# Expert up biases from small loads of three rows, added by four products in four row groups

## The reference, cut to what matters

```python
hcat = xb @ w_up[e] + b_up[e]                  # 128 rows x 1024, w_up 1024 x 2048
y = clamped_swiglu(hcat) @ w_down[e] + b_down[e]   # w_down 1024 x 1024
def clamped_swiglu(hcat):
    gate, lin = hcat[:, :D_EXPERT], hcat[:, D_EXPERT:]
    gate = jnp.minimum(gate, 7.0); lin = jnp.clip(lin, -7.0, 7.0)
    return (lin + 1.0) * (gate * jax.nn.sigmoid(1.702 * gate))
```

## Time and profile before

| | |
|---|---|
| median of 3 runs | 1734.01 us (1733.99 to 1736.2) |
| profiled execution | 1735.64 us, its span 1733.5 us |
| TensorE, VectorE, ScalarE, GpSimd busy | 1637.6, 1478.0, 1103.7, 214.2 us |
| granted clock over the span | 0.975 |
| experts | from about 570 us to the end |

### The profile page before, as it was taken

One profiled execution on the slowest core, in us unless ns is written; L12 is line 12 of the kernel. 1 busy time (PEld: TensorE's weight loads), 2 busy tenths in 40 slices (PEclk: granted clock), 3 DMA queues, 4 the chain that ended last, 5 costly groups with the idle time before them and its releaser, 6 DMA issues.

```text
span 1733.5 us, 33793 instructions
## 1 busy us (share of the span) xinstructions
PE 1637.6 (94%) x12579; PEld 1331.7 (77%) x12580; DVE 1478.0 (85%) x1721; ACT 1103.7 (64%) x1078; POOL 214.2 (12%) x134
## 2 busy tenths in 40 slices
PE   7999899889896999999999999999999999999993
PEld 6778787778675778888888888888888888888882
DVE  5585677676586899999999999999999999999995
ACT  4533425333325777777777777777777777777772
POOL 0001111010103121111211111111211112111110
PEclk9999989999797999999999999999999999999997
DMA  6231101000338999999999999999999999999993
GB/s 200 73 101 55 30 15 30 9 21 15 104 133 279 373 386 365 383 380 378 373 359 385 375 383 372 372 376 375 380 361 376 377 377 375 361 378 377 380 368 111
DMA packets 207631, 473.33 MB, mean 273 GB/s; under 512 B 18701, under 2 KB 29403, under 8 KB 207355
## 3 DMA queue, kind: packets, MB, share of 16 engines
q1 hardware_dynamic: 197179, 442.74, 69.2%
q0 software_dynamic: 9792, 27.28, 7.1%
q10 hardware_dynamic: 576, 2.10, 0.3%
HBM read 454.35 MB, written 26.08 MB: 277 GB/s over the span
## 4 chain that ended last, share of the span: by engine, by line
PE 60%; DMA 4%; DVE 2%; issue 1%; ACT 1%; SPq 0%; DVEq 0%; POOLq 0%; ACTq 0%
PE bank L2183 19%; PE bank L2186 19%; PE bank L2184 18%; PE bank L2209 3%; DMA w_raw<-in_expert_w_up 2%; PE bank L2193 1%; DVE moe_w_lo L2169 1%; ACT moe_w_hi L2165 0%; DMA x<-sum_rows 0%; DMA moe_x_gathered<-hn_rows,moe_gather_rows 0%; DMA sum_rows<-moe_y,moe_scatter_rows 0%; DVE x L2663 0%; DVE moe_x_lo L2220 0%; PE bank L2201 0%; DVE moe_a_lo L2220 0%
## 5 line engine op out<-in xcount | busy, mean ns | idle before, releaser
L2169 DVE TENSOR_TENSOR moe_w_lo<-w_raw,moe_w_hi 128x2048 fp32r<-128x2048 f32 x384 | 867.9, 2287 | 46.7 <-ACT moe_w_hi L2165 45.2
L2165 ACT ACTIVATE moe_w_hi<-w_raw 128x2048 fp32r<-128x2048 f32 x384 | 735.9, 1917 | 124.7 <-PE bank L2186 109.2
L2183 PE MATMUL bank<-moe_w_hi,moe_x_hi 128*128 128x512 f32 x1024 | 406.0, 396 | 0.3 <-DVE moe_w_lo L2169 0.3
L2186 PE MATMUL bank<-moe_w_lo,moe_x_hi 128*128 128x512 f32 x1024 | 400.2, 391 | 0.0
L2184 PE MATMUL bank<-moe_w_hi,moe_x_lo 128*128 128x512 f32 x1024 | 399.6, 390 | 0.0
L2186 PEld LDWEIGHTS bank<-moe_w_lo,moe_x_hi 128*128 128x128 f32 x1024 | 192.6, 188 | 41.0
L2183 PEld LDWEIGHTS bank<-moe_w_hi,moe_x_hi 128*128 128x128 f32 x1024 | 192.7, 188 | 40.2 <-DVE moe_x_lo L2220 1.3
L2184 PEld LDWEIGHTS bank<-moe_w_hi,moe_x_lo 128*128 128x128 f32 x1024 | 192.9, 188 | 38.6
L2183 PE MATMUL bank<-moe_w_hi,moe_a_hi 128*128 128x512 f32 x512 | 208.2, 407 | 1.4 <-DVE moe_a_lo L2220 1.4
L2186 PE MATMUL bank<-moe_w_lo,moe_a_hi 128*128 128x512 f32 x512 | 201.0, 393 | 0.0
L2184 PE MATMUL bank<-moe_w_hi,moe_a_lo 128*128 128x512 f32 x512 | 200.3, 391 | 0.0
(11 more groups left out here) (343 smaller groups left out, 2078.8 us busy)
## 6 DMA issues: line engine op xcount, KB each, us to landing
w_raw<-in_expert_w_up SPq DMA_DIRECT2D x512, 512.0 KB, 8.1
w_raw<-in_expert_w_down SPq DMA_DIRECT2D x256, 512.0 KB, 9.4
proj_w_raw<-in_w_in SPq DMA_DIRECT2D x36, 384.0 KB, 3.3
mixer_bias_table<-in_att_bias SPq DMA_DIRECT2D x16, 256.0 KB, 2.7
x<-in_w_o SPq DMA_DIRECT2D x8, 512.0 KB, 6.6
sum_rows<-x SPq DMA_DIRECT2D x5, 512.0 KB, 4.0
x<-in_x ACTq DMA_DIRECT2D x4, 512.0 KB, 6.7
x<-in_x SPq DMA_DIRECT2D x4, 512.0 KB, 4.0
```

The costliest lines, as they stand in the source:

```text
L2165: act.activation(w_hi[:, j % RING, :], raw[:, j % RAW, :], ACT.Copy).then_inc(hi_w[j % RING], 1)
L2169: eng.tensor_tensor(w_lo[:, j % RING, :], raw[:, j % RAW, :], w_hi[:, j % RING, :].bitcast(F32), ALU.subtract)\
L2183: pe.matmul(out, s_hi[:, k, :], w_hi[:, j % RING, w], start=first, stop=False)
L2186: ins = pe.matmul(out, s_hi[:, k, :], w_lo[:, j % RING, w], start=False, stop=ends)
```

## The change

`biasb` and `selb` are gone. Four small DMAs per expert (`load_bias`, L2199) bring 3 rows of 512 bf16 numbers each to partitions 0, 32, 64 and 96 of a buffer `bias_rows`, of which there are two. One burst of four products (`add_biases`, L2209 of the changed kernel), each over 3 rows in its own group of 32 rows of TensorE, adds them: it closes the banks U00 and U01 of the expert, and opens the banks U10 and U11 of the same expert, whose products come afterwards. The last products of slot 7 close U10 and U11. SyncE waits in each expert n until `actd` is 2n, which is the second half of the activation of expert n - 1, then issues the four loads for expert n + 1, and then the weight loads of expert n.

```diff
@@ slot_matmuls: first product of a bank only where not begun @@
-                    first = k == 0
+                    first = k == 0 and not begun
@@
-        def add_bias(pe, e, B, key, col):
-            pe.matmul(B.tile(key)[:, :], selb[:, ds(e, 1), :].rearrange("p a s -> p (a s)"), biasb[:, col:col + 512],
-                      start=False, stop=True).then_inc(B.fill_sem(key), 1)
+        bias_view = bias_dram.rearrange("(a e) (g c) -> e g a c", a=3, g=4)
+
+        def load_bias(sp, e, buf):
+            for g in range(4):
+                sp.dma_start(brow[32 * g:32 * g + 3, buf, :], bias_view[ds(e, 1), g, :, :].rearrange("e a c -> (e a) c"))\
+                  .then_inc(bias_in[buf], 16)
+
+        def add_biases(pe, buf, loaded, B, it, first, B1, it1, second):
+            pe.wait_ge(bias_in[buf], 64 * loaded)
+            for key in second:
+                pe.wait_ge(B1.free_sem(key), B1.before(it1, key))
+            for Bk, key, g, ends in ((B, first[0], 0, True), (B, first[1], 2, True), (B1, second[0], 1, False),
+                                     (B1, second[1], 3, False)):
+                rows = slice(32 * g, 32 * g + 3)
+                ins = pe.matmul(Bk.tile(key)[:, :], ones[rows, :], brow[rows, buf, :], start=not ends, stop=ends)
+                if ends:
+                    ins.then_inc(Bk.fill_sem(key), 1)
@@ pe_block @@
-                slot_matmuls(pe, n, j, B, it, keys, x_hi, x_lo, 2 * (j - 4))
+                slot_matmuls(pe, n, j, B, it, keys, x_hi, x_lo, 2 * (j - 4), keys if j == 7 else (), True)
-            for i, key in enumerate(keys):
-                add_bias(pe, e, B, key, F * i + 512)
@@
-                for i, key in enumerate(first):
-                    add_bias(pe, e + 1, B, key, F * i)
+                add_biases(pe, 1 - par, it + par + 1, B, it, first, B, it + par, [(1 - par, "U10"), (1 - par, "U11")])
@@ act_block, ahead of the split of slot 11 @@
+            act.wait_ge(B.fill_sem((par, "U11")), B.count(it, (par, "U11")))
+            act.sem_inc(used[3], 1)
@@ SyncE, start of the experts @@
-            sp.dma_start(biasb[:, :], bias_dram).then_inc(bias_in, 16)
-            sp.dma_start(selb[:, :, :], ext["c_selb"].bitcast(BF16).rearrange("p (e s) -> p e s", e=E)).then_inc(bias_in, 16)
+            load_bias(sp, 0, 0)
+            load_bias(sp, 1, 1)
@@
-            with sp.Fori(1, E - 1) as n:
-                load_block(sp, n, n, True)
+            with sp.Fori(0, E // 2 - 1) as i:
+                for q in range(2):
+                    n = 2 * i + 1 + q
+                    sp.wait_ge(actd, 2 * n)
+                    load_bias(sp, n + 1, q)
+                    load_block(sp, n, n, True)
@@ GpSimd, start @@
+            pool.memset(ones[:, :], 1.0).then_inc(ones_set, 1)
```

More of the change, by code:

```diff
@@ L2069, in experts @@
         ident = keep["ident"]
-        posm, meta, over, biasb, selb, iota, lim = (keep[k] for k in ("posm", "meta", "over", "biasb", "selb", "iota", "lim"))
+        posm, meta, over, iota, lim = (keep[k] for k in ("posm", "meta", "over", "iota", "lim"))
         x, dense, counts, order, raw = (keep[k] for k in ("x", "dense", "counts", "order", "w_raw"))
@@ L2091, in experts @@
         fs = sb("final_sums", [P, NT + 1])
+        brow = sb("bias_rows", [P, 2, 512], BF16)
+        ones = sb("ones", [P, P], BF16)
         nov = sb("overflows", [P, E])
@@ L2118, in experts @@
         fw_in = sem("final_w_in")
-        bias_in = sem("bias_in")
+        bias_in = [sem(f"bias_rows_in{b}") for b in range(2)]
+        ones_set = sem("ones_set")
         bd_filled = sem("own_bias_filled")
@@ L2170, in split_lo, with slot_matmuls @@
                .then_inc(lo_w[j % RING], 1)
-        def slot_matmuls(pe, n, j, B, it, keys, s_hi, s_lo, k0, finish=()):
+        def slot_matmuls(pe, n, j, B, it, keys, s_hi, s_lo, k0, finish=(), begun=False):
             pe.wait_ge(lo_w[j % RING], nslot(n, j) + 3)
@@ L2418, in first_pe @@
                 slot_matmuls(pe, 0, j, pro, 0, keys, x_hi, x_lo, 2 * j)
-            pe.wait_ge(bias_in, 32)
-            for i, key in enumerate(keys):
-                add_bias(pe, 0, pro, key, F * i)
+            pe.wait_ge(ones_set, 1)
+            pe.wait_ge(bd_done, NT)
+            add_biases(pe, 0, 1, pro, 0, keys, main, 0, [(0, "U10"), (0, "U11")])
             pe.wait_ge(bd_done, NT)
@@ L2521, in lead_in @@
                     slot_matmuls(eng, n, j, B, it, keys, x_hi, x_lo, 2 * j)
-                for i, key in enumerate(keys):
-                    add_bias(eng, e, B, key, F * i)
+                add_biases(eng, 0, it + E // 2 + 1, B, it, keys, B, it, [(0, "U10"), (0, "U11")])
             if what == "act":
@@ L2599, in _ @@
                         e = sp.value_load(over[0:1, ds(k, 1)], min_val=0, max_val=E - 1)
+                        sp.wait_ge(actd, 2 * (E + k))
+                        load_bias(sp, e, 0)
                         load_lead_in(sp, E + k, e)
@@ L2723, in router_constants @@
     tri = np.concatenate([1.0 * (p[:, None] < p[None, :]), np.ones((P, P))], axis=1)
-    selb = np.zeros((3 * E, E, P))
-    for part in range(3):
-        selb[E * part + np.arange(E), np.arange(E), :] = 1.0
     b16 = lambda v: (v.astype(np.float32).view(np.uint32) >> 16).astype(np.uint16)
-    return {"c_router": rc, "c_lim": lim, "c_tri": b16(tri), "c_selb": b16(selb.reshape(3 * E, E * P)),
+    return {"c_router": rc, "c_lim": lim, "c_tri": b16(tri),
             "c_iota": np.arange(T + P, dtype=np.float32) + 1.0}
@@ L2764, in build @@
         mix_router(nc, psum, ext, keep, hn_dram, acc_dram)
-        for name, shape, dt in (("over", [P, 2 * NOV + 1], I32), ("biasb", [3 * E, 2 * F], BF16), ("selb", [3 * E, E, P], BF16),
-                                ("final_w", [P, D], F32)):
+        for name, shape, dt in (("over", [P, 2 * NOV + 1], I32), ("final_w", [P, D], F32)):
             keep[name] = sb(name, shape, dt)
```

## The result

The changed kernel takes 1862.63 us (median of 4 runs, 1857.56 to 1864.69), the kernel before, on the same chip, 1735.11 us (4 runs, 1733.99 to 1738.07). The ratio is 1.073, 95% interval 1.071 to 1.075. The sign of the forecast was right, its size was half of what came: 1798 was predicted, 64 us more, and it is 128 us more, outside the range.

The account below looks back on a forecast made before the run. Taken as bound by TensorE with the DMA right behind; a turn of 7.2 + 25.0 + 5.7 = 37.9 us, 30 times, against 1073.0 before adds 64 to 1734, giving 1798 us, range 1752 to 1832.

Parts of the forecast that it names:

- S: The DMA's service time per expert, taken as 35.6 us, just under TensorE's 35.72.
- The place of the loss: SyncE's wait before the next expert's first load leaves a DMA queue hole of 2.3 us in every expert.
- T: The moment the second half of an expert's activation ends, for which SyncE waits in the changed kernel.
- I take 5.2, bounds 4.9 and 6.7: Microseconds from issue to landing of the first pair of weight loads behind the wait, on idle DMA engines.
- Worse: Rival: TensorE's clock falls while idling, 1876 us, or the pair takes 6.7 us to land, 1843; chance 0.06.
- From slot 12 to T: From slot 12's landing over ScalarE's split, VectorE's split and the activation to T: 5.7 us a turn.
- TensorE is not in this loop: Claim that the turn from T to T bypasses TensorE, so its saved 0.6 us a turn buys nothing.
- The eight slots: Weight loads queued behind an expert's first load, up to slot 12: 25.0 us of each turn.
- Elsewhere even: Two 1.15 MB start loads gone, about 3 us, against eight small issues added, 2.7 us: even.
- The signs: Expected in the profile: ScalarE's splits wait 1 to 3 us an expert for DMA; SyncE's longest wait at L2199.
- The burst: TensorE's four bias products: 0.30 us replacing 0.90, a gain of 0.6 us an expert, 19 us were TensorE alone.
- Nothing moves: Rival: the queue's hole is just filled and the DMA's S caps the gain, 1731 to 1734 us; chance 0.05.

Follow-up runs that it names:

- e5: Kernel before with every w_down load cut to 768 of its 1024 columns, not computing the layer's result: 1731.46 us.
- e2: Changed kernel with SyncE waiting for the first half of the activation instead of the second, and the burst's products reordered: 1735.71 us.
- e4: Changed kernel with the loads of slots 4, 5 and 6 issued ahead of SyncE's wait and the four bias loads: 1737.86 us.
- e9: Changed kernel with the loads of two slots, 4 and 5, issued ahead of SyncE's wait and the bias loads: 1738.95 us.
- e6: e2 with every w_down load cut to 768 of its 1024 columns, not computing the layer's result: 1714.17 us.
- e1: Kernel before plus only SyncE's wait for the second activation half ahead of an expert's first weight load, biases as before: 1807.01 us.
- e12: e1 with slot 4 loaded alone, the loads of slot 5 and all behind held until slot 4 has landed: 1940.61 us.
- e7: e6 with all four products of the burst reading rows 0 to 2, so in one row group: 1737.05 us.
- e8: Changed kernel with the load of one slot, slot 4, issued ahead of SyncE's wait and the bias loads: 1789.32 us.
- e10: Kernel before plus SyncE's wait for the second activation half, placed behind the load of slot 4, biases as before: 1733.36 us.

## Why the prediction was right, and where it was wrong

**What bounds the kernel now: right.** TensorE with the DMA right behind. Less work for the DMA alone (e5) or for TensorE alone (e2, e4, e9) leaves the time within 0.4% of before; less for both lowers it (e6). S, taken as 35.6, is 35.8 to 35.9 in e2, e4 and e9.

**The place of the loss: right.** It is the loop through SyncE's wait. The wait alone makes 72 us (e1); three slots queued ahead of it take all but 3 us away (e4). The bias loads harm through their 1.8 us of SyncE's time behind the wait, not through the DMA (e2, e4). The Trainium skill (DMA: Bandwidth & Descriptors, "Rules for kernel authors") speaks against small transfers for their overhead on the DMA; e2 has all of them and takes no longer, and their packets take 0.04 us an expert, so here that price isn't on the path.

**Cost of a bias load's issue: right.** 0.45 was taken, 1.8 for four; from T to the weight issue it is 2.06 for 1.99.

**"I take 5.2, bounds 4.9 and 6.7": the step that failed.** The pair lands 7.0 us after its issue in the turn shown, 6.85 in the mean, beyond the upper bound. The value was put together from a lone load of 384 KB, 3.2 us, and bytes at the full rate. The row that was right stood beside it: the start at 544.1, 6.7 us, dismissed as the cold start of the weights, though each hole in the queue is such a start. In its place: 1.4 us until the first packet, two at 280 GB/s, and 0.6 for sharing with the loads behind (e12). It makes 1.6 of the 2.3 us by which a turn was too short, 30 × 1.6 = 48 us. The rival "Worse" had this price, 1843, and a chance of 0.06 together with the clock; it deserved far more.

**From slot 12 to T: 5.7 was too small, 6.4 measured,** 0.7 a turn, 21 us. Slot 12 lands at 1028.7, but ScalarE begins its split at 1029.41, behind X1, and X1 waits for TensorE, which waited for VectorE:

```profile
1027.49 0.68 DVE L2237 TENSOR_TENSOR moe_x_lo<-bank,moe_x_hi 128x512 fp32r<-128x512 f32 x1
```

```profile
1028.23 0.66 PE L2226 MATMUL bank<-ident,moe_x_gathered 128*128 128x128 f32 x4 [3.55 <-DVE moe_x_lo L2237]
```

```profile
1028.92 0.60 ACT L2231 ACTIVATE moe_x_hi<-bank 128x512 fp32r<-128x512 f32 x1 [0.99 <-PE bank L2226]
1029.41 1.90 ACT L2168 ACTIVATE moe_w_hi<-w_raw 128x2048 fp32r<-128x2048 f32 x1
```

The 5.7 is what the way takes when X1 is not late. So it is in 8 of the 30 turns (5.67 to 5.69); one is the turn whose slot 12 lands at 868.4 and whose T is 874.08:

```profile
867.53 0.58 ACT L2231 ACTIVATE moe_x_hi<-bank 128x512 fp32r<-128x512 f32 x1
868.50 1.91 ACT L2168 ACTIVATE moe_w_hi<-w_raw 128x2048 fp32r<-128x2048 f32 x1 [0.39 <-DMA w_raw<-in_expert_w_up]
```

In the other 22 turns X1 ends after slot 12 has landed, and the way takes 6.3 to 6.9. The forecast's "TensorE is not in this loop" was therefore not quite so: its transposition is, though not its products.

**The eight slots: right,** 24.9 for 25.0. **Elsewhere even: off by 5 us,** to the good: expert 0's T came 4.7 us earlier. Together 48 + 21 - 5 is 64, the whole miss. **The signs:** SyncE's longest wait and the hole behind T are where the forecast put them; but the splits wait for loads for (117.9 + 21.9) / 15 = 9.3 us an expert (1000 to 1600 us), where it said 1 to 3.

**The burst: right in kind, dearer than taken.** 0.30 was taken. Four products in four row groups take 0.33 us, and with the 0.09 ahead of them 0.42; so the gain is 0.90 - 0.42 = 0.48 an expert instead of 0.6, 15 us, and e6 against e5 gives 0.49 an expert, 17.3 us in all. That it needs distinct row groups is shown by e7. The Trainium skill (TensorEngine Tiling (Array Packing), "Key Properties") says that a change of the tiling mode drains the array; the rows agree, with 0.32 to the burst's start where 0.23 is usual, and with the same 0.32 in e7; that it is a drain they don't show.

**The clock.** The forecast said 1.00. After the 3.55 us without work TensorE ran at its lower level (1.2 GHz):

```profile
1026.00:1028.00 2.00, 0.00 (x0) 0.00 (x0) 2.00 (x2) 1.91 (x1) 0.00 (x0) 1.00 1.05 392
1028.00:1030.00 2.00, 1.77 (x8) 1.48 (x9) 2.00 (x3) 1.08 (x2) 0.00 (x0) 0.71 1.06 397
1030.00:1032.00 2.00, 2.00 (x6) 1.55 (x5) 2.00 (x3) 1.80 (x2) 0.00 (x0) 0.50 1.03 410
1032.00:1034.00 2.00, 2.00 (x10) 1.62 (x9) 2.00 (x2) 0.68 (x1) 0.00 (x0) 0.94 1.03 410
```

A mean of 0.71, 0.50 and 0.94 in three stretches of 2 us is 1.2, 2.0 and 0.2 us at 0.50, together 3.4. Behind it ScalarE waits 1.5 and 0.8 us for TensorE at slots 13 and 14, which are behind slot 12 and so outside the loop; how much of this is the clock and how much TensorE's late start isn't separated. To the way from slot 12 to T the clock adds next to nothing: in four turns it is 1.00 in the 20 us ahead of T (815.0 to 834.9, for one), and they take 6.4 to 6.6 us, like the others with a late X1.

**Rival "Nothing moves" is what the change does once the hole is covered:** e2, e4 and e9 stand at ratios of 1.0007, 1.0018 and 1.0034, none under 1. No version that computes the result is faster than the kernel before: e10's 1733.36 and e2's 1735.71 are no different from it.

## What to carry to other kernels

A wait in the queue of an engine that issues loads costs what the DMA queue doesn't hold at that moment: count the work that is still queued when the wait ends, in microseconds, add the next slot's own pitch, and compare the sum with the time from the end of the wait to the next slot's landing. With the bias loads that time is here 2 + 7 us: two slots queued, 6.8 + 2.7, were enough (e9), one, 4.1 + 2.7, was not (e8). Without them it is 0.3 + 7 us, and one slot, 0.5 us short by this count, cost nothing (e10). Put the wait, and small loads, behind as much. Where two engines are in balance, saving on one shows only if the other is relieved: try the saving in a kernel that leaves out some of the other's work before judging it. When bounding a transfer on idle engines, take the row of an actual start with the same loads, not a smaller load plus bytes at the full rate.

## What was not expected of the hardware

- After a hole in the queue the 16 engines don't come back at full rate: 1.4 us until the first packet, then 280 GB/s (e12), and 383 to 403 only from 8 us after the issue (changed kernel). Why the rate is low at first stays open; that the loads behind take part in it explains 0.6 us and no more.
- From issue to landing a slot of 1 MB takes 7.0 us even if another is under way at its issue (e8).
- Going from a product over 128 rows to the products over 3 rows costs TensorE 0.09 us, in four row groups (changed kernel) as in one (e7), and going back about as much: the last of e7's four products, which start 0.22 us apart, is followed by the next instruction only after 0.31.
- Behind 3.55 us without work TensorE was granted its lower clock, 1.2 GHz, for 3.4 us. To the way from slot 12 to T it added next to nothing.
